# Moving the token parts from 128 to 352 modulo 512 bytes of a partition, with everything behind them at the same place modulo 512

## The reference

```
x = first_block(x, ...)    # two layers, each:
    h = rmsnorm(x); p = h @ w_in                       # 1024 -> 3328 columns
    branches = rwkv7(p), stick_breaking(p), retention(p), conformer_conv(p)
    x += (sum_i sigmoid(h @ w_gate[i]) * (branches[i] @ w_branch[i])) @ w_out
    h = rmsnorm(x)
    x += swiglu(h)         # layer 0: dense, hidden width 2816
    x += top-2-of-8 experts, each a swiglu of hidden width 1408   # layer 1
x = second_block(x, ...)   # recurrent block + swiglu; then keys/values, sparse attention + swiglu
```

## Time and profile before

| | before |
|---|---|
| median of 3 runs | 1833.4 us (1833.2 to 1836.06) |
| the profiled execution's own time | 1836.3 us |
| its span, first to last instruction | 1834.5 us |
| TensorE busy, share of the span | 98% |
| granted TensorE clock, mean | 0.993 of 2.4 GHz |
| HBM read | 360.03 MB |

### The profile page before, as it was taken

One profiled execution on the slowest core, in us unless ns is written; L12 is line 12 of the kernel. 1 busy time (PEld: TensorE's weight loads), 2 busy tenths in 40 slices (PEclk: granted clock), 3 DMA queues, 4 the chain that ended last, 5 costly groups with the idle time before them and its releaser, 6 DMA issues.

```text
span 1834.5 us, 30118 instructions
## 1 busy us (share of the span) xinstructions
PE 1793.0 (98%) x12734; PEld 1551.6 (85%) x12734; DVE 1357.7 (74%) x1533; ACT 1012.6 (55%) x1220; POOL 127.6 (7%) x167
## 2 busy tenths in 40 slices
PE   8999999999999999999999999999999999899999
PEld 8988898888899889788888888795888898668887
DVE  5967667856586776699999999886867565758674
ACT  6663346433566425477777777666534456765331
POOL 0010000201001000000000000000112000001110
PEclk9999999999999999999999999999999999799999
DMA  7432346553443235489999999644654344026451
GB/s 287 146 111 100 118 181 238 186 199 123 172 162 116 94 115 186 197 335 355 349 365 358 348 348 360 228 162 187 223 188 170 127 165 157 1 78 258 164 221 59
DMA packets 52268, 364.13 MB, mean 198 GB/s; under 512 B 5921, under 2 KB 6049, under 8 KB 9761
## 3 DMA queue, kind: packets, MB, share of 16 engines
q1 hardware_dynamic: 50832, 357.43, 52.5%
q0 software_dynamic: 1296, 4.72, 0.7%
HBM read 360.03 MB, written 2.10 MB: 197 GB/s over the span
## 4 chain that ended last, share of the span: by engine, by line
PE 56%; DVE 4%; ACT 3%; issue 2%; DMA 1%; ACTq 0%; DVEq 0%
PE banks L1510 55%; ACT work L896 1%; DMA ring<-weights_in 1%; DVE ring_lo L2619 1%; PE banks L2228 1%; ACT tokens L896 0%; ACT L896 0%; PE banks L2495 0%; DVE work L3502 0%; DVE small L3504 0%; DVE tokens L2686 0%; DMA more<-weights_in 0%; PE banks L2174 0%; DVE work L3051 0%; ACT high L896 0%
## 5 line engine op out<-in xcount | busy, mean ns | idle before, releaser
L1510 PE MATMUL banks<-tokens,high 128*128 128x256 f32 (+1 forms) x2576 | 548.7, 304 | 3.6 <-DVE tokens L2686 2.7
L1510 PE MATMUL banks<-tokens,ring_lo 128*128 128x256 f32 x1664 | 466.0, 280 | 0.0
L1510 PEld LDWEIGHTS banks<-tokens,high 128*128 128x128 f32 x2576 | 411.8, 188 | 32.6 <-issue 9.7
L2619 DVE TENSOR_TENSOR ring_lo<-ring,high 128x2048 fp32r<-128x2048 f32 (+1 forms) x153 | 347.9, 2281 | 65.6 <-ACT high L896 63.8
L896 ACT ACTIVATE high<-ring 128x2048 fp32r<-128x2048 f32 (+1 forms) x155 | 292.9, 1894 | 71.0 <-DMA ring<-weights_in 69.1
L1510 PEld LDWEIGHTS banks<-tokens,ring_lo 128*128 128x128 f32 x1664 | 313.1, 188 | 0.1
L896 ACT ACTIVATE work<-banks 128x512 f32<-128x512 f32 (+7 forms) x139 | 80.5, 584 | 244.7 <-PE banks L1510 239.0
L2619 DVE TENSOR_TENSOR more_lo<-more,more_high 128x2048 fp32r<-128x2048 f32 (+1 forms) x86 | 188.6, 2203 | 30.0 <-ACT more_high L896 29.8
L1510 PE MATMUL banks<-tokens,more_high 128*128 128x512 f32 x592 | 206.8, 393 | 0.5 <-DVE tokens L2686 0.5
L896 ACT ACTIVATE more_high<-more 128x2048 fp32r<-128x2048 f32 (+1 forms) x86 | 158.3, 1843 | 68.7 <-DMA more<-weights_in 68.6
L896 ACT ACTIVATE glu<-scr 128x256 f32<-128x256 f32 x66 | 27.7, 419 | 218.2 <-DVE scr L2653 218.2
(11 more groups left out here) (297 smaller groups left out, 2996.8 us busy)
## 6 DMA issues: line engine op xcount, KB each, us to landing
ring<-weights_in SPq DMA_DIRECT2D x225, 1024.0 KB, 4.9
more<-weights_in SPq DMA_DIRECT2D x104, 1024.0 KB, 5.8
more<-weights_in SPq DMA_DIRECT2D x8, 512.0 KB, 4.0
ring<-weights_in SPq DMA_DIRECT2D x6, 512.0 KB, 4.4
consts<-consts_in SPq DMA_DIRECT2D x1, 1682.0 KB, 16.2
params<-params_in SPq DMA_DIRECT2D x1, 1162.5 KB, 10.9
x<-x_in SPq DMA_DIRECT2D x2, 512.0 KB, 3.9
normed_rows<-scr POOLq DMA_DIRECT2D x2, 512.0 KB, 10.2
```

Source lines behind the costliest of these rows:

```text
L1510: return pe.matmul(out_, lhsT, rhs, start=start, stop=stop, **kw)
L2619: tt(lo_of(g), ring_of(g), hi_of(g).bitcast(F32), SUB).then_inc(unit_lo, 1)
```

## The change

`sb(name, shape)` lays a tensor at the next free place of the partition. The change adds a tensor `align` of 56 floats (224 bytes) behind x, which nothing reads or writes, makes the pad of `tokens` 96 floats instead of 24, and lets the experts' views begin 96 floats into `tokens` instead of 24.

```diff
         x = sb("x", [P, TT, D])
+        sb("align", [P, 56])
         with ExitStack() as shared:
             hT = shared.enter_context(nc.sbuf_tensor("hT", [P, KT, T], F32))
-        tokens = sb("tokens", [P, 2 * KT * T + 24], F32R)
+        tokens = sb("tokens", [P, 2 * KT * T + 96], F32R)
         h_parts = tokens[:, 0:2 * KT * T].rearrange("p (i k t) -> p i k t", i=2, k=KT)
         h_hi, h_lo = h_parts[:, 0, :, :], h_parts[:, 1, :, :]
...
         CUT = KT * CAP
-        input_parts = tuple(grid(tokens[:, 24 + CUT * i:24 + CUT * i + CUT], KT) for i in range(2))
-        result_parts = tuple(tokens[:, 24 + CUT * i:24 + CUT * i + CUT] for i in (2, 3))
+        input_parts = tuple(grid(tokens[:, 96 + CUT * i:96 + CUT * i + CUT], KT) for i in range(2))
+        result_parts = tuple(tokens[:, 96 + CUT * i:96 + CUT * i + CUT] for i in (2, 3))
```

## The result

| | before | changed |
|---|---|---|
| median, runs of both in turn (20 each) | 1835.07 us (1831.73 to 1841.09) | 1839.42 us (1836.1 to 1842.75) |
| ratio changed to before | | 1.0022 (95% interval 1.0016 to 1.0029) |
| profiled execution's own time, its span | 1836.3, 1834.5 us | 1836.1, 1834.3 us |

What follows compares the result with a forecast made beforehand. The prediction took TensorE's pace in dense runs as the bound. Its terms, 6.3 + 2.6 + 0 - 0.6 - 0.4 = +7.9 us, on a median of 1833.4 gave 1841.3 us, with a range of 1820 to 1850.

Steps and rivals of the forecast that it cites:

- What bounds the kernel: TensorE, busy 98% of the span; what counts is the time between matmul starts inside dense runs.
- the first term of the sum: Projections and gates: 3168 matmuls of 256 columns go from 118.0 to 120.0 ns, +6.3 us.
- The 118.0 for before: Projections and gates at offset -96: mean pace taken for 3168 matmuls, from stretches at 117.3, 118.7 and 120.0 ns.
- Feed-forward, 256 columns, +2.6: Dense feed-forward stages: 1056 matmuls with low weight parts go from 117.5 to 120.0 ns, +2.6 us.
- nearest-offset step: For large classes moved to +128: take 120.0 ns, the pace at +96, the nearest offset with a row.
- Feed-forward, 512 columns in two runs, 0, bounds -3.0 and +5.3: Dense feed-forward stages, 1056 matmuls over h_hi and h_lo: 0 taken, as the bounds have opposite signs.
- `token_tiles`, -0.6: 288 matmuls, tokens stationary, 256 weight columns moving, at offset -128: 120.0 to 118.0 ns, -0.6 us.
- Absorbed, -0.4: Start of the recurrent block, 384 matmuls: a weight DMA on the chain hides some of 0.8 us, 0.4 taken off.
- The rival "faster": Dense runs: operands' reads collide less at 128 bytes; 256 columns at 114.6 ns, -16.8 us, 1816.6 us; chance 34%.

Runs made afterwards that it cites:

- views_left: Changed kernel without its last edit: the experts' views begin 24 floats into `tokens` as before; ratio 1.0042 to the kernel before (1.0028 to 1.0057).
- The sweep: Model left out, TensorE alone at sixteen moving-minus-stationary offsets; 117.3 ns a matmul of 256 columns at -96, 118.6 at +128; pairs 346.7 and 351.1 ns.
- minus128: Changed kernel with the token parts 256 bytes further down (offset -128), experts' views unmoved; ratio 1.0024 to the kernel before (1.0014 to 1.0034).
- narrow_only: Changed layout, only projections, gates, `token_tiles` and keys at offset +128, feed-forward layers at -96; ratio 1.0008 to the kernel before (0.9996 to 1.0019).
- feed_only: Changed layout, only the feed-forward layers at offset +128, projections, gates and keys at -96; ratio 1.0029 to the kernel before (1.0019 to 1.0039).

## Why the prediction was right, point by point

- **What bounds the kernel: right.** The time followed the paces of TensorE's dense runs in every kernel here, in direction and to within some us. Even in the experts' stage, with its DMA share of 0.9, 3.5 of 3.9 us of pace arrived (views_left).
- **The step that was mis-sized is the first term of the sum,** 3168 x (120.0 - 118.0) = +6.3 us. By the starts of all of them the mean went from 118.1 to 118.7 ns: 3168 x 0.6 = +1.9 us. What was wrong in it is the sentence that took 120.0 for +128, since the "nearest offset with a row is +96": the period is 256 bytes, so +128 is also -128, lies as near to -96 as to +96, and has a pace of its own, 118.6, between theirs. The sweep shows it, and minus128 has the time and the pair's pace again. 120.0 does occur at +128 in some stretches of other kernels (narrow_only), but in none of the 76 stretches of the changed kernel. The 118.0 for before was right (118.1).
- **Feed-forward, 256 columns, +2.6:** 117.51 to 120.39 ns, +3.0 us. Right in size, but by the same nearest-offset step that failed in the projections, so in part by luck: at one offset, +128, the 256 columns take 118.7 ns in groups of three and 120.4 inside a pair.
- **Feed-forward, 512 columns in two runs, 0, bounds -3.0 and +5.3:** 229.3 to 230.6 ns, +1.4 us, inside its bounds. Both together are +4.4, as are the six halves, and feed_only alone gives the whole slowdown (+5.3).
- **`token_tiles`, -0.6:** 119.9 to 118.6 ns, -0.4 us. Right.
- **Absorbed, -0.4:** 1.9 + 3.0 + 1.4 - 0.4 = 5.9 us of pace against about 4 measured (2.9 to 5.3), so more went missing than the 0.4 taken off. Where is open. In the profiled pair the experts' stage is 0.9 us shorter and the recurrent block 0.6, but single profiles do not settle it: the experts' paces are the same in both, and over the eight profiles that leave them at offset 0 the stage takes 411.1 to 414.3 us, 414.3 and 412.0 in the two of one kernel. The four of the changed layout are the shorter ones (411.1 to 411.8); no run says why.
- **The rival "faster":** that the two operands' places against each other cost time is shown, that it is their reads is not; a better place exists, but at 64 bytes and not at 128; its price of 16.8 us was for a pace of 114.6, and of the eight offsets only -64 gets under that.
- The comparison with one profile would have misled: the attention's 3.3 us at another granted clock are as large as the effect.

## What to carry to other kernels

Where TensorE is the bound with a new stationary operand for each float32r matmul, the place of the moving against the stationary operand in the partition was worth up to 2% (pairs) to 6% (256 columns) of the pace in the sweep; measure it with a sweep of the kernel's own patterns, since what is best for 256 columns (-64 bytes) is among the worst for the pair with two runs (353 against 347 ns). If two stages want different places, give them two views of one buffer. Do not interpolate between offsets by distance before the period is known, and look at stages rather than spans when an effect is as small as the difference of two executions.

## What the runs showed of the hardware that was not expected

- The pace of split float32r matmuls depends on the two operands' offset with a period of 256 bytes: 113.3 to 120.0 ns for 256 columns, 226.7 (offset 0) to 234.3 for 512 in one run, 346.7 to 353.3 for the pair. The figures 113.3, 120.0, 226.7, 346.7 and 353.3 come out as whole numbers of cycles of 1.2 GHz (136, 144, 272, 416, 424); 234.3 does not (281.2). Several offsets have more than one pace, so this is a table of paces seen, and not the only one for each.
- The Trainium skill, page "TensorE: Matmul & The Clock Gate", "Back-to-back issue gap", has N/2.4 + 2.5 ns as the isolated gap. With a stationary operand of its own for each matmul the least here was 113.3 for N = 256 (an estimate by the formula: 109.2) and 226.7 for N = 512 (215.8). In "Step-by-step: what each phase is for" the two reads have ports of their own and take nothing from each other; the dependence of the pace on their offset, 113.3 to 120.0 ns, speaks against that for this type, though no run here looks at the reads themselves.
- At offsets 192 and 32 two paces are stable (113.3 and 117.8, 116.7 and 117.8), at -96 the whole kernels have three (117.3, 118.7, 120.0), and a dense run keeps the one it starts in until it is broken. What picks the pace, and what the two operands' accesses share, is not settled by these runs.
